# The adaLN slabs of a hybrid decoder layer between the slabs of its input projection, on one Trainium2 core

## The chip, the cores and the metric

The kernel runs on one core of a Trainium2 chip. The metric is device time in microseconds (us) of a whole call, a launch of one program; the median of several runs is given. The profile is that of one execution, and durations below are taken from it. Engines are named as in the profile: PE is TensorE (its matmuls; PEld is its weight load), DVE is VectorE, ACT is ScalarE, POOL is GpSimd, SP is SyncE, whose queue issues the weight loads. L560 is line 560 of the kernel; after the change the same code stands some 17 to 20 lines further down.

## The reference

One inference step of two layers. Each layer normalises its input, modulates it with rows of adaLN (a product of a condition vector with `w_ada`), projects it once (`w_in`), runs four mixers on the parts of that projection, and projects their results back (`w_out`); a feed-forward or experts follow. Cut to what matters here:

```python
def trunk_layer(x, mod, g_mix, g_ffn, lp, past, ffn):
    sh1, sc1, gt1, sh2, sc2, gt2 = [m[:, None, :] for m in jnp.split(mod.astype(x.dtype), 6, axis=-1)]
    h = rmsnorm(x, g_mix) * (1 + sc1) + sh1
    y, state = token_mixers(h, lp, past)
    x = x + gt1 * y
    h = rmsnorm(x, g_ffn) * (1 + sc2) + sh2
    x = x + gt2 * ffn(h)
    return x, state

# in token_mixers:  proj = h @ lp['w_in'];  ...four mixers (SSD, FoX, gated delta rule, MoBA)...;  y = y @ lp['w_out']
# in reference:     xp, sp = trunk_layer(xp, cp @ w_ada[l] + b_ada[l], ...)   and the same for the samples
```

The model width is 1024; `w_ada` has 6 x 1024 columns per layer. The prompt has 256 tokens, and eight samples bring one token each: 264 columns in the projection. The samples attend to cached pages of keys and values.

## The kernel before

**Slabs and the ring.** All large weights come through a ring of four slots (`ring0` to `ring3`). `plan_stream` writes the order of the loads as a list. Each entry is a slab with the number of ticks that its use makes. A tick is an increment of `tile_done`, which TensorE makes when a piece of work that reads a slab is over. SP goes through the list in order; `slab(i)` waits until the slab that held the slot before has made its last tick, then issues the load. So SP's queue is in order, and a slab that waits holds up all behind it. A program chooses the slot of each slab ahead of time, by who was used longest ago.

**The input projection.** `project` multiplies 26 tiles, 128 columns of `w_in` each, from nine slabs (`IN_SLABS`). Eight slabs hold three tiles and the third one, slab 2, holds two; they are 1.5 and 1.0 MB. A tile is 24 matmuls (L747, L748, L749): weights and input are each split into a high and a low part. ScalarE makes the high part from the ring (`in_high`, L1388), VectorE the low part (L1877). `IN_SPLITS` = 3 tiles are split ahead: in `drain`, ScalarE first splits tile j + 3 and then copies the result of tile j out of its bank (L1471). Two banks of PSUM alternate. Between tiles TensorE also runs small pieces (`sums` and `rows_fox` after tile 7, `head_norms` after tiles 13, 20 and 24), and VectorE runs the convolutions.

**An adaLN block.** A slab of `w_ada` (2 MB, 512 columns) is used by `ada_unit`, in two halves ("units") of 16 k-steps and column groups each, so that a block is 2 units; the trace has it as 64 records of L667. It writes bank 0. ScalarE copies that to `mrow` (`mod_rows`), TensorE transposes `mrow` into bank 1 (`ada_turn`, L676), ScalarE copies this on into `modT` (`mod_columns`). `ada_fill(l, place)` runs the units that the table `ADA_UNITS` gives a place, and ahead of each block the turn of the one before it; `ada_drain` does the copies at the same place of ScalarE's program. What a block makes is wanted only by the end of the mixers, by the feed-forward and by the next layer.

**What follows the projection.** The places are, in order, `gdn` (gated delta rule), `chain` (its last step), `ssd`, then `att0` to `att7`, the eight heads of attention of the prompt. Into the heads the samples' work is woven: `state_rows` (L982), `value_rows` (L990), `key_sums` (L996), `state_outputs` (L1005), `cache_bias`. For each head TensorE computes the scores (`score`, L953 and L954), VectorE reads them and makes the weights (`shares`, L2083 to L2085), TensorE turns them (`turn_shares`, L644) and multiplies the values (`values`, L970 to L972). The cache pages come through the same ring: `k` (two loads of a page set, without a tick) and `v`, and in the samples' attention they are used.

Before the change layer 0 has 1 block at `gdn`, 1 at `chain`, 2 at `ssd` and 1 at each of `att0` to `att6`; layer 1 has 1, 1, 1 and 1 at each of `att0` to `att3`.

Of the kernel before, what the change touches and what calls it, by code (L numbers as in the profile page):

```python
# [30 lines left out]
P = 128  # L31
# [5 lines left out]
DEPTH = 2  # L37
# [23 lines left out]
NSLOT = 4  # L61
# [17 lines left out]
def consts():  # L79
# [49 lines left out]
    {"gdn": 2, "chain": 2, "ssd": 4, **{f"att{n}": 2 for n in range(7)}, "att7": 0},  # L129
    {"gdn": 2, "chain": 2, "ssd": 2, **{f"att{n}": 2 for n in range(4)}, **{f"att{n}": 0 for n in range(4, 8)}}]  # L130
# [11 lines left out]
def plan_stream():  # L142

    out = [("ada", 0, (c,), 1) for c in range(MIX_CHUNKS)]
    for l in range(DEPTH):
        if l:
            out += [("ada",) + (NORM_ADA["mix", l][0], (NORM_ADA["mix", l][1],), 1)]
        out += [("in", l, s, s[1] // P) for s in IN_SLABS]
        ada = [("ada", la, (c,), 1) for la, c in MIXER_ADA[l]]
        out += ada[:NSLOT] + [("k", l, (m,), 0) for m in range(2)] + ada[NSLOT:] + [("v", l, (m,), 1) for m in range(2)]  # L150
        out += [("out", l, (c,), 4) for c in range(2)]
        if l == 0:
            out += [("ada",) + (NORM_ADA["ffn", l][0], (NORM_ADA["ffn", l][1],), 1)]
            out += [("gu", l, (c,), 4) for c in range(FF // 256)]
            out += [("down", l, (c, h), 4) for c in range(4) for h in range(2)]
    return out

def build(nc, A, O, const_at, NCONST):
    ctx = ExitStack()  # L160
    with ctx:
# [346 lines left out]

        class Order:
# [119 lines left out]
        def _(pe):  # L629
# [29 lines left out]
            def ada_unit(l, c, half):  # L659

                w = ring[slot_of[index[("ada", l, c)]]][:, :].rearrange("p (k n) -> p k n", k=KD)
                if half == 0:
                    use(index[("ada", l, c)])
                b = fill(0, "mod_rows") if half == 0 else bank[0]
                for k in range(4 * half, 4 * half + 4):
                    for j in range(4):
                        ins = mm(b[j * QUAD:(j + 1) * QUAD, 0:P], cT[:, k, :], w[:, k, j * P:(j + 1) * P],  # L667
                                 start=k == 0, stop=k == KD - 1)
                if half:
                    tick(ins)  # L670

            def ada_turn(l, c):

                o.need("mod_rows")
                b = fill(1, "mod_ready")
                pe.transpose(b[:, 0:P], mrow[:, :], C("ident")).then_inc(sem("mod_turned"), 1)  # L676
# [74 lines left out]
            def project(l, first, n):  # L751

                for t in range(first, first + n):
                    s, m = in_tiles[t]
                    if m == 0:
                        pe.wait_ge(landed[slot_of[index[("in", l) + s]]], landed_at[index[("in", l) + s]])
                    o.need("in_w_low", 1 if t else 3)
                    b = fill(tiles[0] % 2, "tile_copied")
# [278 lines left out]
            def attention(l):  # L1037
# [5 lines left out]
                for n in range(8):  # L1043
# [7 lines left out]
                    ada_fill(l, f"att{n}")  # L1051
# [286 lines left out]
            for l in range(DEPTH):  # L1338
# [19 lines left out]
                project(l, 25, 1)  # L1358
                gdn_beta_rows()
# [23 lines left out]
        def _(act_e):  # L1383
# [15 lines left out]
            def mod_rows(l, c):  # L1399
# [3 lines left out]
                copy(mrow[:, :], bank[0][:, 0:P], "mod_rows")  # L1403

            def mod_columns(l, c):
                o.need("mod_turned")
                copy(modT[:, 4 * c:4 * c + 4, :], bank[1][:, 0:P].rearrange("p (m j) -> p m j", m=4)[:, :, 0:9], "mod_ready")
# [45 lines left out]
            def in_high(l, t):  # L1453
# [4 lines left out]
                if t >= IN_SPLITS:  # L1458
                    act_e.wait_ge(tile_done, ticks_before(index[("in", l) + IN_SLABS[0]]) + t + 1 - IN_SPLITS)
                copy(win_high[:, t % IN_SPLITS, :, :], in_tile(l, t), "in_w_high")  # L1460

            def drain(l, first, n):
                i0 = ticks_before(index[("in", l) + IN_SLABS[0]])
                for j in range(first, first + n):
                    if j + IN_SPLITS < TILES:
                        in_high(l, j + IN_SPLITS)
                    act_e.wait_ge(tile_done, i0 + j + 1)
                    b = bank[(i0 + j) % 2]
# [20 lines left out]
            for l in range(DEPTH):  # L1489
# [63 lines left out]
                drain(l, 25, 1)  # L1553
                head_roots()
# [76 lines left out]
                for n in range(8):  # L1631
# [4 lines left out]
                    ada_drain(l, f"att{n}")  # L1636
# [959 lines left out]
```

## Time and profile before

| | |
|---|---|
| runs | 1411.69, 1418.78, 1423.9 us |
| median | 1418.78 us |
| span of the profiled execution | 1419.1 us |
| PE busy | 1301.8 us (92%) |
| PEld busy | 1126.2 us (79%) |
| DVE busy | 941.5 us (66%) |
| ACT busy | 707.7 us (50%) |
| DMA | 326.76 MB, 230 GB/s in the mean |

"Busy" is a share of the whole span and so a mean over stages with different limits; which engine a stage waits for is seen only when the span is cut. The chain that ended last is the work followed back from the last instruction, at each step to what released it. The input projection lies from 44 to 134 us in layer 0 and from 556 to 646 us in layer 1, the heads of attention and the samples' work within them from 207 to 281 us and from 715 to 780 us.

### The profile page before, as it was taken

To read this page: it belongs to the slowest core of one execution; us is meant where nothing else is said; L and a number is where in the kernel's file an instruction comes from. 1 tells how busy PE (TensorE), PEld (TensorE's weight loads), DVE (VectorE), ACT (ScalarE), POOL (GpSimd) and SP (SyncE) were. 2 spreads that over 40 slices of the span, in tenths; PEclk is the share of its full clock that TensorE was granted. 3 is DMA by queue.
4 is the path that set the end of the run, shared out by engine and by line. 5 is a ranking of instruction groups with operands and counts; after the bars stand their busy time and mean duration, and the time that the engine had idled before them with its cause. 6 is when DMAs were issued, how large, how long until landed. Compare 5 with 4: busy or idle time off the path is not lost.

```text
span 1419.1 us, 25438 instructions
## 1 busy us (share of the span) xinstructions
PE 1301.8 (92%) x10487; PEld 1126.2 (79%) x10487; DVE 941.5 (66%) x1612; ACT 707.7 (50%) x1188; POOL 10.1 (1%) x22
## 2 busy tenths in 40 slices
PE   4999898987999998998888878999999999999994
PEld 3899756766999997998666657888887979797984
DVE  1675635624555545676358247898899899989986
ACT  2566222214444444563132125776677677767772
POOL 0000000000000000000000000000000000000000
PEclk9999877588999999999776888999999999999997
DMA  9545358553444443456265523898889889979991
GB/s 388 213 154 207 121 183 318 180 215 149 178 179 141 164 186 130 175 202 202 62 226 163 188 110 125 324 358 304 320 336 347 301 324 351 335 281 343 349 339 39
DMA packets 30332, 326.76 MB, mean 230 GB/s; under 512 B 6018, under 2 KB 6530, under 8 KB 8066
## 3 DMA queue, kind: packets, MB, share of 16 engines
q1 hardware_dynamic: 28738, 319.17, 61.3%
q0 software_dynamic: 1472, 5.89, 1.1%
q8 instruction: 86, 1.41, 0.4%
q14 instruction: 36, 0.29, 0.1%
HBM read 319.15 MB, written 5.89 MB: 229 GB/s over the span
## 4 chain that ended last, share of the span: by engine, by line
PE 81%; DVE 9%; DMA 4%; ACT 3%; issue 3%; SPq 0%; DVEq 0%; POOL 0%; ACTq 0%; POOLq 0%
PE bank L747 19%; PE bank L748 18%; PE bank L749 18%; PE bank L1132 4%; DMA ring<-in_w_ada 4%; PE bank L667 3%; PE bank L803 2%; PE bank L1226 2%; PE bank L644 1%; PE bank L699 1%; DVE w_low L2400 1%; DVE win_low L1877 1%; PE bank L1254 1%; PE bank L1005 1%; PE bank L770 1%
## 5 line engine op out<-in xcount | busy, mean ns | idle before, releaser
L2400 DVE TENSOR_TENSOR w_low<-ring,w_high 128x1024 fp32r<-128x1024 f32 x352 | 399.6, 1172 | 46.0 <-ACT w_high L1756 44.5
L1756 ACT ACTIVATE w_high<-ring 128x1024 fp32r<-128x1024 f32 x352 | 342.2, 1016 | 15.1 <-PE bank L749 13.9
L747 PE MATMUL bank<-w_high,hcH 128*128 128x512 f32 x448 | 184.9, 413 | 2.3 <-DVE w_low L2400 1.9
L749 PE MATMUL bank<-w_low,hcH 128*128 128x512 f32 x448 | 176.2, 393 | 0.0
L748 PE MATMUL bank<-w_high,hcL 128*128 128x512 f32 x448 | 176.0, 393 | 0.0
L747 PE MATMUL bank<-w_high,hidH 128*128 128x256 f32 x448 | 128.5, 287 | 3.0 <-DVE w_low L2400 3.0
L749 PE MATMUL bank<-w_low,hidH 128*128 128x256 f32 x448 | 126.7, 283 | 0.0
L748 PE MATMUL bank<-w_high,hidL 128*128 128x256 f32 x448 | 126.7, 283 | 0.0
L747 PE MATMUL bank<-pH,win_high 128*128 128x264 f32 x416 | 119.9, 288 | 2.5 <-issue 2.0
L1388 ACT ACTIVATE arena<-bank 128x264 f32<-128x264 f32 (+8 forms) x128 | 51.7, 407 | 137.7 <-PE bank L644 51.9
L748 PE MATMUL bank<-pH,win_low 128*128 128x264 f32 x416 | 117.9, 283 | 0.0
L749 PE MATMUL bank<-pL,win_high 128*128 128x264 f32 x416 | 117.8, 283 | 0.0
L747 PEld LDWEIGHTS bank<-w_high,hcH 128*128 128x128 f32 x448 | 84.4, 188 | 37.2 <-DVE w_low L2400 22.4
L747 PE MATMUL bank<-hH,w_high 128*128 128x264 f32 x352 | 101.1, 287 | 5.0 <-DVE w_low L2277 5.0
L1388 ACT ACTIVATE w_high<-ring 128x1024 fp32r<-128x1024 f32 (+1 forms) x76 | 71.5, 944 | 63.3 <-PE bank L749 63.3
L748 PE MATMUL bank<-hH,w_low 128*128 128x264 f32 x352 | 100.8, 286 | 0.0
L749 PE MATMUL bank<-hL,w_high 128*128 128x264 f32 x352 | 100.7, 286 | 0.0
L749 PEld LDWEIGHTS bank<-w_low,hcH 128*128 128x128 f32 x448 | 84.3, 188 | 18.9
L2277 DVE TENSOR_TENSOR w_low<-ring,w_high 128x1024 fp32r<-128x1024 f32 (+1 forms) x76 | 80.0, 1081 | 28.0 <-ACT w_high L1388 28.0
L748 PEld LDWEIGHTS bank<-w_high,hcL 128*128 128x128 f32 x448 | 84.7, 189 | 13.1
L1877 DVE TENSOR_TENSOR win_low<-ring,win_high 128x1024 fp32r<-128x1024 f32 x52 | 62.9, 1222 | 42.2 <-ACT win_high L1388 30.1
L747 PEld LDWEIGHTS bank<-w_high,hidH 128*128 128x128 f32 x448 | 85.8, 192 | 3.9 <-issue 3.9
(393 smaller groups left out, 2548.5 us busy)
## 6 DMA issues: line engine op xcount, KB each, us to landing
ring<-in_moe_gu SPq DMA_DIRECT2D x56, 2048.0 KB, 8.6
ring<-in_moe_down SPq DMA_DIRECT2D x32, 1792.0 KB, 7.6
ring<-in_w_ada SPq DMA_DIRECT2D x24, 2048.0 KB, 8.9
ring<-in_w_in SPq DMA_DIRECT2D x16, 1536.0 KB, 6.5
ring<-in_ffn_gu SPq DMA_DIRECT2D x11, 2048.0 KB, 7.6
ring<-in_ffn_down SPq DMA_DIRECT2D x8, 1408.0 KB, 5.8
ring<-in_w_out SPq DMA_DIRECT2D x4, 2048.0 KB, 7.7
ring<-in_cache_fox_k SPq DMA_DIRECT2D x32, 128.0 KB, 3.0
```

The source lines that it names most:

```text
L667: ins = mm(b[j * QUAD:(j + 1) * QUAD, 0:P], cT[:, k, :], w[:, k, j * P:(j + 1) * P], start=k == 0, stop=k == KD - 1)
L747: mm(out, wh, xh, start=start, stop=False)
L748: mm(out, wl, xh, start=False, stop=False)
L749: return mm(out, wh, xl, start=False, stop=stop)
L803: ins = mm(b[q, h * HD:(h + 1) * HD], lhs(q, g * H + h), rhs(q, g * H + h), start=True, stop=True)
L1132: ins = mm(b[:, 0:NT], w[:, k, m * P:(m + 1) * P], yT[:, k, :], start=k == 0, stop=k == KD - 1)
L1226: ins = mm(bank[6 + part][:, i * 2 * CAP:(i + 1) * 2 * CAP], (htokH, htokL)[part][:, g, k * P:(k + 1) * P], G[:, g, :, :], start=g == 0, s ...
L1388: o.go(A_(out, in_, ACT.Copy), name)
L1756: A_(split(w_high), src, ACT.Copy).then_inc(sem("w_high_ready"), 1)
L1877: v(TT(win_low[:, t % IN_SPLITS, :, :], in_tile(l, t), win_high[:, t % IN_SPLITS, :, :], ALU.subtract), "in_w_low")
L2277: v(TT(split(w_low), src, split(w_high), ALU.subtract), "split_low")
L2400: TT(split(w_low), src, split(w_high), ALU.subtract).then_inc(sem("w_low_ready"), 1)
```

## The change

The blocks leave the heads. Nine places `in0` to `in8` in the projection stand for its slabs; in layer 0 a block is run after each of slabs 1 to 8, in layer 1 after each of slabs 1 to 7; in0 has none. Layer 0 keeps one block at each of `gdn`, `chain` and `ssd`, layer 1 keeps none outside the projection. In `plan_stream` the slabs of `w_ada` stand between those of `w_in` in the same order, and the rest of them follow; the pages `k`, that stood behind the fourth adaLN slab, come after the last of them, ahead of `v`. In `ada_banks` the blocks within the projection get banks 6 and 7 for their rows and turns, the others keep 0 and 1. `in_tick` works out ScalarE's ticks anew, since the blocks' ticks now stand among those of the tiles, and the bank of a tile follows the tile's number.

```diff
 ADA_UNITS = [
-    {"gdn": 2, "chain": 2, "ssd": 4, **{f"att{n}": 2 for n in range(7)}, "att7": 0},
-    {"gdn": 2, "chain": 2, "ssd": 2, **{f"att{n}": 2 for n in range(4)}, **{f"att{n}": 0 for n in range(4, 8)}}]
+    {**{f"in{n}": 2 for n in range(1, 9)}, "gdn": 2, "chain": 2, "ssd": 2},
+    {**{f"in{n}": 2 for n in range(1, 8)}, "in8": 0, "gdn": 0, "chain": 0, "ssd": 0}]
...
-        out += [("in", l, s, s[1] // P) for s in IN_SLABS]
         ada = [("ada", la, (c,), 1) for la, c in MIXER_ADA[l]]
-        out += ada[:NSLOT] + [("k", l, (m,), 0) for m in range(2)] + ada[NSLOT:] + [("v", l, (m,), 1) for m in range(2)]
+        for n, s in enumerate(IN_SLABS):
+            out += [("in", l, s, s[1] // P)]
+            k = ADA_UNITS[l][f"in{n}"] // 2 if n else 0
+            out += ada[:k]
+            ada = ada[k:]
+        out += ada + [(kind, l, (m,), t) for kind, t in (("k", 0), ("v", 1)) for m in range(2)]
         out += [("out", l, (c,), 4) for c in range(2)]
...
+        def in_tick(l, t):
+
+            s_, m = in_tiles[t]
+            return ticks_before(index[("in", l) + s_]) + m + 1
+
+        def ada_banks(l, c):
+
+            own = next(m for m in range(DEPTH) if (l, c) in MIXER_ADA[m]) if (l, c) in sum(MIXER_ADA, []) else None
+            if own is None:
+                return 0, 1
+            inside = sum(ADA_UNITS[own].get(f"in{n}", 0) for n in range(1, 9)) // 2
+            return (6, 7) if MIXER_ADA[own].index((l, c)) < inside else (0, 1)
...
                 for t in range(first, first + n):
                     s, m = in_tiles[t]
+                    if t and m == 0 and IN_SLABS.index(s) > 1:
+                        ada_fill(l, f"in{IN_SLABS.index(s) - 1}")
...
-                    ada_fill(l, f"att{n}")
...
                 project(l, 25, 1)
+                ada_fill(l, "in8")
                 gdn_beta_rows()
...
                 if t >= IN_SPLITS:
-                    act_e.wait_ge(tile_done, ticks_before(index[("in", l) + IN_SLABS[0]]) + t + 1 - IN_SPLITS)
+                    act_e.wait_ge(tile_done, in_tick(l, t - IN_SPLITS))
...
                 for j in range(first, first + n):
+                    slab_n = IN_SLABS.index(in_tiles[j][0])
+                    if in_tiles[j][1] == 0 and slab_n > 1:
+                        ada_drain(l, f"in{slab_n - 1}")
                     if j + IN_SPLITS < TILES:
                         in_high(l, j + IN_SPLITS)
...
                 drain(l, 25, 1)
+                ada_drain(l, "in8")
                 head_roots()
...
-                    ada_drain(l, f"att{n}")
```

`ada_unit`, `ada_turn`, `mod_rows` and `mod_columns` now take their bank from `ada_banks`.

In SP's queue at the start of layer 0's projection, the loads of slabs 0 to 8 of `w_in` and of the first blocks before the change (the width of a row is the number of elements per partition: 3072 is a slab of three tiles, 4096 a slab of `w_ada`):

```order
L560 DMA ring0<-in_w_in 128x3072
L560 DMA ring1<-in_w_in 128x3072
L560 DMA ring2<-in_w_in 128x2048
L560 DMA ring3<-in_w_in 128x3072
L540 DMA arena<-in_conv 128x240
L560 DMA ring0<-in_w_in 128x3072
L560 DMA ring1<-in_w_in 128x3072
L560 DMA ring2<-in_w_in 128x3072
L560 DMA ring3<-in_w_in 128x3072
L560 DMA ring0<-in_w_in 128x3072
L557 DMA ring1<-in_w_ada 128x4096
L557 DMA ring2<-in_w_ada 128x4096
```

The same place after it:

```order
L577 DMA ring0<-in_w_in 128x3072
L577 DMA ring1<-in_w_in 128x3072
L574 DMA ring2<-in_w_ada 128x4096
L577 DMA ring3<-in_w_in 128x2048
L557 DMA arena<-in_conv 128x240
L574 DMA ring0<-in_w_ada 128x4096
L577 DMA ring1<-in_w_in 128x3072
L574 DMA ring2<-in_w_ada 128x4096
L577 DMA ring3<-in_w_in 128x3072
L574 DMA ring0<-in_w_ada 128x4096
L577 DMA ring1<-in_w_in 128x3072
```

Of the four slots two now go round among the slabs of `w_in` and two among those of `w_ada`: the fourth slab of `w_in` reuses the slot of the second.

On TensorE, where tile 5 of layer 0's projection ends and tile 6 begins (slab 1 to slab 2), the rows after the change; before it the tiles follow on each other here without another row between L749 and L747:

```order
L765 MATMUL bank<-pH,win_high 128x264
L766 MATMUL bank<-pH,win_low 128x264
L767 MATMUL bank<-pL,win_high 128x264
L685 MATMUL bank<-ring,cT 32x128 x32
L765 MATMUL bank<-pH,win_high 128x264
L766 MATMUL bank<-pH,win_low 128x264
L767 MATMUL bank<-pL,win_high 128x264
```

The block (L685, both units in one row) stands between the tiles; from the next slab on the turn of the block before it (L694) stands ahead of each.

On TensorE in layer 0's heads 3 and 4, before the change (L990 is `value_rows`, L996 `key_sums`):

```order
L676 MATMUL bank<-cst,mrow 128x128
L667 MATMUL bank<-ring,cT 32x128 x32
L990 MATMUL bank<-arena,cst 64x128 x16
L644 MATMUL bank<-cst,arena 128x128 x3
L970 MATMUL bank<-arena 64x128
L971 MATMUL bank<-arena 64x128
L972 MATMUL bank<-arena 64x128
L953 MATMUL bank<-arena 128x128
L954 MATMUL bank<-arena 128x256
L676 MATMUL bank<-cst,mrow 128x128
L667 MATMUL bank<-ring,cT 32x128 x32
L996 MATMUL bank<-arena,cst 128x512 x2
```

And after it:

```order
L1010 MATMUL bank<-arena,cst 64x128 x16
L661 MATMUL bank<-cst,arena 128x128 x3
L990 MATMUL bank<-arena 64x128
L991 MATMUL bank<-arena 64x128
L992 MATMUL bank<-arena 64x128
L973 MATMUL bank<-arena 128x128
L974 MATMUL bank<-arena 128x256
L1016 MATMUL bank<-arena,cst 128x512 x2
```

Turn and block (L676, L667) are gone from between the scores of a head and the samples' work; the rest stands as it was.

## Rows read from the trace of the kernel before

**Rows 1.** Page, part 4: the chain that ended last, by engine and line.

```profile
PE 81%; DVE 9%; DMA 4%; ACT 3%; issue 3%; SPq 0%; DVEq 0%; POOL 0%; ACTq 0%; POOLq 0%
```

**Rows 2.** Windows: us; busy PE, PEld, DVE, ACT, POOL (instructions); PEclk, DMA share, GB/s.

```profile
44.40:133.80 89.40, 88.16 (x704) 86.30 (x703) 54.74 (x99) 54.02 (x113) 1.22 (x2) 1.00 0.44 162
44.40:61.65 17.25, 17.25 (x144) 17.25 (x143) 8.03 (x18) 7.61 (x18) 0.67 (x1) 1.00 0.27 98
207.03:245.54 38.51, 32.35 (x416) 23.14 (x416) 22.68 (x81) 10.18 (x37) 0.91 (x2) 0.81 0.80 295
245.54:280.70 35.16, 33.19 (x262) 25.76 (x262) 25.17 (x39) 9.18 (x29) 0.17 (x1) 0.50 0.56 173
715.09:753.04 37.95, 30.76 (x351) 21.37 (x351) 22.88 (x81) 9.80 (x35) 0.91 (x2) 0.77 0.60 204
753.04:780.25 27.21, 25.04 (x138) 19.61 (x138) 25.18 (x39) 8.21 (x25) 0.17 (x1) 0.56 0.51 152
```

**Rows 3.** Timeline of TensorE: start us, busy us, what, [idle ahead <-releaser].

```profile
139.84 1.95 PE L667 MATMUL bank<-ring,cT 128*32 128x128 f32 x64
...
237.20 0.33 PE L676 MATMUL bank<-cst,mrow 128*128 128x128 f32 x1
```

**Rows 4.** Timeline of TensorE and VectorE in layer 1's mixers, `gdn` and `chain`.

```profile
658.63 1.15 PE L803 MATMUL bank<-cst,arena 64*64 64x64 f32 x32 [1.66 <-DVE arena L1980]
...
693.82 3.64 PE L667 MATMUL bank<-ring,cT 128*32 128x128 f32 x64
...
700.63 0.55 PE L920 MATMUL bank<-arena 128*64 128x128 f32 x6
...
695.63 0.42 DVE L2034 TENSOR_TENSOR arena<-arena 64x256 f32<-64x256 f32 x1
```

**Rows 5.** Timeline of VectorE just behind layer 0's projection.

```profile
137.91 0.69 DVE L1951 TENSOR_TENSOR arena<-arena,bank 128x512 f32<-128x512 f32 x1 [1.32 <-ACT arena L1559]
```

**Rows 6.** Timeline of ScalarE in layer 0's projection, after tile 5.

```profile
62.16 1.06 ACT L1388 ACTIVATE win_high<-ring 128x1024 fp32r<-128x1024 f32 x1 [1.55 <-PE bank L749]
63.13 0.36 ACT L1471 ACTIVATE arena<-bank 128x256 f32<-128x256 f32 x1
```

**Rows 7.** Page, part 6 (us to landing), and L560's five loads of 53 to 90 us.

```profile
ring<-in_w_ada SPq DMA_DIRECT2D x24, 2048.0 KB, 8.9
...
DMA to landing us min/median/max: 6.1/6.6/7.3
```

**Rows 8.** Timeline of TensorE and VectorE around tile 14 of layer 0.

```profile
92.30 0.36 PE L747 MATMUL bank<-pH,win_high 128*128 128x264 f32 x1 [1.01 <-issue]
...
90.97 1.23 DVE L1877 TENSOR_TENSOR win_low<-ring,win_high 128x1024 fp32r<-128x1024 f32 x1 [3.79 <-ACT arena L1388]
...
94.12 1.22 DVE L1877 TENSOR_TENSOR win_low<-ring,win_high 128x1024 fp32r<-128x1024 f32 x1
```

**Rows 9.** Waits of VectorE in 207 to 245.54: us in total, times, longest.

```profile
DVE arena L2142 <- PE bank L996: 8.8, 2, 8.7
...
DVE arena L2121 <- PE bank L982: 4.1, 1, 4.1
```

**Rows 10.** Timeline of TensorE in heads 3 to 5, layer 0, then layer 1.

```profile
235.07 0.55 PE L644 MATMUL bank<-cst,arena 128*128 128x128 f32 x3
235.55 0.43 PE L970 MATMUL bank<-arena 128*64 128x128 f32 x2
...
239.55 1.98 PE L996 MATMUL bank<-arena,cst 128*128 128x512 f32 x4
...
246.43 0.69 PE L970 MATMUL bank<-arena 128*64 128x128 f32 x2
...
247.90 0.79 PE L953 MATMUL bank<-arena 64*128 64x128 f32 x2
...
743.04 1.96 PE L990 MATMUL bank<-arena,cst 8*64 8x128 f32 x32
```

**Rows 11.** Chain of waits within layer 0's heads: start us, us, what.

```profile
227.74 9.89 DMA ring<-in_w_ada
```

More of the change, by code:

```diff
@@ L663, in ada_unit @@
                     use(index[("ada", l, c)])
-                b = fill(0, "mod_rows") if half == 0 else bank[0]
+                rb = ada_banks(l, c)[0]
+                b = fill(rb, "mod_rows") if half == 0 else bank[rb]
                 for k in range(4 * half, 4 * half + 4):
@@ L674, in ada_turn @@
                 o.need("mod_rows")
-                b = fill(1, "mod_ready")
+                b = fill(ada_banks(l, c)[1], "mod_ready")
                 pe.transpose(b[:, 0:P], mrow[:, :], C("ident")).then_inc(sem("mod_turned"), 1)
@@ L757, in project @@
                     o.need("in_w_low", 1 if t else 3)
-                    b = fill(tiles[0] % 2, "tile_copied")
+                    b = fill(t % 2, "tile_copied")
                     wh, wl = win_high[:, t % IN_SPLITS, :, :], win_low[:, t % IN_SPLITS, :, :]
@@ L1402, in mod_rows @@
                 act_e.wait_ge(tile_done, ticks_before(i) + 1)
-                copy(mrow[:, :], bank[0][:, 0:P], "mod_rows")
+                copy(mrow[:, :], bank[ada_banks(l, c)[0]][:, 0:P], "mod_rows")
             def mod_columns(l, c):
                 o.need("mod_turned")
-                copy(modT[:, 4 * c:4 * c + 4, :], bank[1][:, 0:P].rearrange("p (m j) -> p m j", m=4)[:, :, 0:9], "mod_ready")
+                copy(modT[:, 4 * c:4 * c + 4, :], bank[ada_banks(l, c)[1]][:, 0:P].rearrange("p (m j) -> p m j", m=4)[:, :, 0:9], "mod_ready")
             def ada_drain(l, place):
@@ L1458, in in_high @@
                 if t >= IN_SPLITS:
-                    act_e.wait_ge(tile_done, ticks_before(index[("in", l) + IN_SLABS[0]]) + t + 1 - IN_SPLITS)
+                    act_e.wait_ge(tile_done, in_tick(l, t - IN_SPLITS))
                 copy(win_high[:, t % IN_SPLITS, :, :], in_tile(l, t), "in_w_high")
             def drain(l, first, n):
-                i0 = ticks_before(index[("in", l) + IN_SLABS[0]])
                 for j in range(first, first + n):
+                    slab_n = IN_SLABS.index(in_tiles[j][0])
+                    if in_tiles[j][1] == 0 and slab_n > 1:
+                        ada_drain(l, f"in{slab_n - 1}")
                     if j + IN_SPLITS < TILES:
                         in_high(l, j + IN_SPLITS)
-                    act_e.wait_ge(tile_done, i0 + j + 1)
-                    b = bank[(i0 + j) % 2]
+                    act_e.wait_ge(tile_done, in_tick(l, j))
+                    b = bank[j % 2]
                     kind, i = dst_of[l][j]
```

## The prediction

> **What bounds the kernel now.** I read the page's chain of waits first: 81% of the chain that ended last is TensorE, 4% the loads of adaLN slabs [rows 1]. That is a mean over stages with different limits, so I cut the span by stage. In layer 0's input projection TensorE is busy 88.2 of 89.4 us at the full clock (2.4 GHz), and the DMA queues only 0.44 [rows 2]: whatever is put on TensorE there must be paid. In the attention heads it is otherwise. I cut them at VectorE's own work: from its first read of a score to the end of `shares(3)` (first half), and from there to the row maxima of the cache scores (second half). First halves: 38.51 us in layer 0 and 37.95 in layer 1, VectorE busy 22.7 and 22.9; second halves: 35.16 and 27.21, VectorE busy 25.2 in both [rows 2]. The granted clock there is 0.81, 0.50, 0.77 and 0.56, a mixture of the two levels, 1.2 and 2.4 GHz. The second half of layer 1 has no adaLN block, that of layer 0 has two; otherwise they run the same program. So the change takes work from a stage where VectorE should be the bound, and puts it into one where TensorE is.
>
> **What is added: the projection.** A block (two units, 64 records) takes 1.95 us at the full clock, the turn of the block before it 0.33 [rows 3]; at the half clock a block takes 3.64 [rows 4]. Layer 0 gets eight blocks in its projection, layer 1 seven. The first has no turn: seven cost 1.95 + 6 x 2.28 = 15.6 us per layer on an engine that had nothing free.
>
> The eighth block of layer 0 stands behind the last tile, where ScalarE is the path: it reads the tile, takes roots, and its exponentials (L1559) release VectorE at 137.91, after VectorE has waited 1.32 us for them [rows 5]. It now has to copy the block's rows before the roots, so it waits for turn and block, 2.28, and copies for some 0.1, less the tile's own copy, 0.36 [rows 6], which lies beside: +2.0. Layer 1 has none there.
>
> **A new wait.** The ring has four slots. A slab of w_in now waits for the one two before it, not four. It lands 6.1 to 7.3 us after its issue, 6.6 in the median [rows 7]. ScalarE splits a tile three ahead *before* it empties the present bank: 1.06 us of split, then about 0.5 of copy [rows 6]. For slabs of three tiles this just fits: the slab is issued at t; TensorE runs a block (2.28) and two tiles of 24 matmuls, 0.12 us apart (144 in 17.25, [rows 2]), 2.88 each, and asks for the bank at t + 8.0; ScalarE hands it over at t + 6.6 + 1.06 + 0.4 = t + 8.1. But slab 2 has two tiles, so the split for slab 3 stands ahead of the copy of slab 1's last tile, and the slot of slab 3 is freed by that same tile. TensorE asks for the bank after a block and one tile, t + 1.95 + 2.88 = t + 4.8, and gets it at t + 6.6 + 1.06 + 0.5 = t + 8.2: +3.3 us in each layer. Behind ScalarE's wait stand VectorE's remainders of the split, and behind those the convolutions; with a block per slab they have some 2 us more than now and are not late.
>
> Against this TensorE has a little free time: 1.0 us ahead of tile 14, and from there to tile 17 it follows VectorE, whose splits come 3.15 us apart against 2.88 for a tile [rows 8]. A block before tiles 14 and 17 fills the first hole, four times 0.27, and some after it: −2.4 per layer. Per layer the projection so grows by 15.6 + 3.3 − 2.4 = 16.5; I add 1.0 in all for loads that land somewhat later because the queue now carries 2 MB more per slab. In all, layer 0: 18.5, layer 1: 16.5, and 1.0.
>
> **What is taken away before the heads.** `gdn` keeps its block in layer 0 and loses it in layer 1; there TensorE stands still for 1.66 us just after, until VectorE's mask (L1980) releases it [rows 4], so a block taken out ahead only lengthens that wait: 0. Layer 0's `ssd` goes from two blocks to one: −2.3 (turn and block). Layer 1 loses `chain` and `ssd`. The first runs at the half clock to 697.4, but what follows needs VectorE, which is ready only at 696.05; then come 1.8 us of TensorE's own work (L905, L644, turn), so the next step starts at about 697.85 in place of 700.63 [rows 4]: −2.8. `chain` of layer 0 is as before.
>
> **What is taken away in the heads.** Second half of layer 0: without its two blocks it should take what layer 1's takes: 35.16 − 27.21 = −8.0. Layer 1's stays.
>
> First halves: VectorE's own 22.8 us plus the waits that remain. The greatest of layer 0 is 8.7 us for the key sums of the delta rule in head 4 [rows 9]. They stand behind `turn_shares`, `values`, `score` and, so far, a block. Without it, at the full clock, `turn_shares` takes 0.5 us (235.07 to 235.55), `values` and `score` together 1.65 (to 237.20, [rows 3]) and the first of two sums 1.0, half of 1.98 [rows 10]; at the half clock `values` takes 1.5 (246.43 to 247.90), and all of it I put at 6.0. VectorE has 1.1 us of its own to do meanwhile, by an estimate. So it waits some 2.1 us at the full clock and 4.9 at the half one. At the half clock `value_rows`, 1.96 us at the full one [rows 10] and so 3.9, also ends after the shares are ready, by an estimate of 2.2; then 0.4 or 1.3 for the second sum. With 1.7 to 2.3 us of small waits for `state_rows`, an estimate from the 4.1 that the longest of them takes with a block ahead [rows 9]: 22.8 + 2.5 + 1.7 = 27.0 at the full clock, 22.8 + 8.4 + 2.3 = 33.5 at the half one. Before, 38.51 and 37.95. Which clock? With blocks it was 0.81 and 0.77; the heads with less work, 0.50 and 0.56 [rows 2]. I take a value in between, 31.0: −7.5 and −7.0.
>
> The rule that speaks against the change: the Trainium skill ("TensorE: Matmul & The Clock Gate", part 1) says that the throttled state is the default and that activity releases it, so that filler taken out of a waiting engine leaves it slow. By this all heads would run at 1.2 GHz, 33.5 us each, and the sum would be 5 us more. The rows bear it out only in part: two blocks in layer 0's second half did not lift 0.50.
>
> **The cache pages.** They now follow all adaLN slabs. The k pages wait for slots of blocks that are over by the end of the projection; they are wanted only in head 5, so both sides of the bound are nothing. The v pages and the slabs of w_out come earlier and are waited for by nobody. The loads that TensorE waited for in the heads (9.9 us from issue to landing on the chain, [rows 11]) lie within the first halves and are gained above, not twice.
>
> **The sum**, against the profiled execution's span of 1419.1 us, 0.3 above the runs' median of 1418.78: layer 0: 18.5 − 2.3 − 7.5 − 8.0 = +0.7. Layer 1: 16.5 − 2.8 − 7.0 = +6.7. With 1.0: +8.4. The feed-forward and the experts are untouched. Predicted: 1427 us.
>
> **The rivals.**
> *Heads at the full clock* (not slower). If TensorE, with less to do but less to wait for, keeps 2.4 GHz, first halves take 27.0: another −8, 1419 to 1420; and if the second halves' score chains go too, 2 us less in each, near VectorE's 25.2: 1416. For it: 0.81 and 0.77 with long stretches at the full clock. Against: 0.50 and 0.56 in second halves. Chance 0.27.
> *Heads at the half clock*: a TensorE that mostly waits falls to 1.2 GHz in all heads; first halves 33.5, +5: 1432. For it: layer 1's bare second half at 0.56. Chance 0.2, and I count it with the likeliest below, since it differs by less than a measurement can tell. (It is the rule of the Trainium skill named above.)
> *Slabs land late* (slower). If w_in slabs take the time of loads that share the queue, 9.9 us [rows 11] in place of 6.6, the bank comes 3.3 us late at each slab from 3 to 8, five more times in both layers and once more at slab 3: about 6 x 3.3 x 2 = 40 less what a longer period leaves the queue; +15 to +35: 1442 to 1462. It decides from a landing of 6.9 us on, the last that hides. Against it: a block's slab of 2 MB (8.9 us in the median, [rows 7]) is issued some 9 us before the next w_in slab and so has just landed. Chance 0.15.
> *The blocks hide in the projection* (faster): then some 30 us of additions fall and the time is near 1395. Against it: TensorE busy 88.2 of 89.4 us at the full clock [rows 2]. Chance 0.05.
>
> **How the numbers follow.** The likeliest, a mixed to low clock in the heads and slabs that land in time: 0.53 with the half clock, its own range 1421 to 1434. Heads at the full clock 0.27, slabs late 0.15, hidden 0.05. For 8 in 10: from 1411, below the full-clock case's 1416 by its unknowns, to 1443, where the late slabs begin. A measurement of this kernel tells about 1% (14 us). Faster than 1405: the hidden blocks and a little of the full clock: 0.08. Slower than 1433: late slabs 0.15, and 0.15 of the half clock with later landings: 0.30. Same: 0.62.
>
> **What would show it.** Right: projection of layer 0 from first tile to last 105 to 107 us instead of 89.4; TensorE idle about 3 us after tile 6 of each layer, with ScalarE's split waiting for a slab; L1559's successor 2 us later; heads without loads on the chain, first halves 27 to 34 us, second halves 27. Wrong: w_in slabs that land later than 7.5 us; second half of layer 0 above 29; a clock in the projection below 1.0; or waits for k pages in heads 5 to 7.

## The result, and the profile of the changed kernel

The changed kernel takes 1432.21 us in the median of its runs (1426.74 to 1435.8), the kernel before 1418.78. The ratio is 1.0103, with a 95% interval of 1.008 to 1.0126: slower by 1%, 13.4 us by the medians. The prediction was 1427 us, 1411 to 1443.

The profiled execution has a span of 1431.2 us. I cut it at the same places as before: the projection from its first tile to the first row of `gdn_beta_rows`, the first half of the heads from VectorE's first read of a score to the end of `shares(3)`, the second half from there to the row maxima of the cache scores. First the windows of the change that answer to [rows 2] (us; busy PE, PEld, DVE, ACT, POOL with their instructions; PEclk, DMA share, GB/s), layer 0, then layer 1:

```profile
42.65:152.08 109.43, 105.99 (x1223) 101.89 (x1221) 54.87 (x101) 56.17 (x130) 1.22 (x2) 0.98 0.72 275
...
215.74:247.79 32.05, 26.79 (x91) 16.50 (x91) 22.48 (x81) 8.23 (x27) 0.90 (x2) 0.53 0.25 70
247.79:275.00 27.21, 25.23 (x132) 19.47 (x132) 25.18 (x40) 8.23 (x25) 0.18 (x1) 0.50 0.26 97
550.73:660.85 110.12, 105.41 (x1159) 101.58 (x1157) 55.82 (x102) 55.65 (x126) 1.09 (x2) 0.97 0.63 232
...
732.38:764.74 32.36, 27.54 (x91) 16.52 (x91) 22.65 (x81) 8.23 (x27) 0.91 (x2) 0.57 0.04 16
764.74:791.94 27.20, 24.81 (x136) 19.66 (x137) 25.17 (x39) 8.30 (x25) 0.17 (x1) 0.56 0.05 20
```

The projections went from 89.4 us to 109.4 and 110.1. The first halves fell to 32.1 and 32.4, and TensorE's granted clock there is now 0.53 and 0.57, against 0.81 and 0.77 with the blocks. Layer 0's second half takes what layer 1's takes, 27.2.

The whole of it by stages, cut from the first and last rows of TensorE and VectorE (the last column is a second execution of the changed kernel, an experiment below):

| us | before | changed | changed, again |
|---|---|---|---|
| start to layer 0's first tile | 44.40 | 42.65 | 42.09 |
| layer 0: projection | 89.40 | 109.43 | 111.30 |
| gdn, to the chain | 33.48 | 33.08 | 33.84 |
| chain | 16.69 | 12.57 | 16.49 |
| chain's block, ssd, to `decode_spread` | 21.07 | 16.02 | 19.71 |
| heads, first half | 38.51 | 32.05 | 32.04 |
| heads, second half | 35.16 | 27.21 | 27.20 |
| layer 1: projection | 89.42 | 110.12 | 110.44 |
| gdn, to the chain | 34.23 | 33.49 | 34.71 |
| chain | 13.33 | 17.05 | 13.89 |
| ssd, to `decode_spread` | 19.62 | 19.01 | 18.40 |
| heads, first half | 37.95 | 32.36 | 31.57 |
| heads, second half | 27.21 | 27.20 | 27.21 |

What is not in the table moved by less than 1 us in the first execution. In sum layer 0 gained 5.8 us, 1.75 of it ahead of its first tile, and layer 1 lost 17.0.

The new wait stands where it was looked for. TensorE in layer 0 between tile 6 and tile 7 and for a while after, then the same place of layer 1 (start, us busy, what, [idle ahead <- releaser]):

```profile
64.91 0.28 PE L766 MATMUL bank<-pH,win_low 128*128 128x264 f32 x1
...
68.36 0.56 PE L765 MATMUL bank<-pH,win_high 128*128 128x264 f32 x1 [3.05 <-ACT arena L1408]
68.72 0.42 PE L766 MATMUL bank<-pH,win_low 128*128 128x264 f32 x1
...
71.30 0.29 PE L766 MATMUL bank<-pH,win_low 128*128 128x264 f32 x1
...
577.29 0.56 PE L765 MATMUL bank<-pH,win_high 128*128 128x264 f32 x1 [3.90 <-ACT arena L1408]
```

ScalarE at that place of layer 0 (L1408 splits, L1493 copies the bank; they were L1388 and L1471):

```profile
66.82 1.06 ACT L1408 ACTIVATE win_high<-ring 128x1024 fp32r<-128x1024 f32 x1 [7.95 <-DMA ring<-in_w_in]
67.78 0.37 ACT L1493 ACTIVATE arena<-bank 128x256 f32<-128x256 f32 x1
```

ScalarE waits 7.95 us for slab 3, splits its first tile, and only then empties the bank that TensorE wants for tile 7. TensorE stands still for 3.05 us, in layer 1 for 3.90. And then there is something that the prediction did not have: a matmul behind the wait takes 0.42 us until 71, and 0.29 after it. The granted clock was 1.00 ahead of the wait and 0.50 when TensorE started again, so the next work ran at 1.2 GHz.

The loads of w_in (six per layer, from issue to landing) were hardly slower than the 6.1, 6.6 and 7.3 of [rows 7]; layer 0, then layer 1:

```profile
L577 SPq DMA_DIRECT2D ring<-in_w_in x6: 327/328/332, 60.4 to 122.6; - x6
...
DMA to landing us min/median/max: 6.1/6.4/7.5
```

```profile
L577 SPq DMA_DIRECT2D ring<-in_w_in x6: 327/328/328, 568.4 to 633.9; - x6
...
DMA to landing us min/median/max: 6.1/6.7/7.6
```

### The profile page after: what moved, and what is told of

The parts are those of the page before. It is cut to its first block, busy times and chain, and to the rows that moved or that the text cites. A ratio compares the mean times of both kernels' runs of the same rounds, so it can differ in the third digit from the quotient of the medians.

```text
span 1431.2 us, 25436 instructions
## 1 busy us (share of the span) xinstructions
PE 1308.0 (91%) x10487; PEld 1130.4 (79%) x10487; DVE 941.6 (66%) x1612; ACT 705.0 (49%) x1188; POOL 10.1 (1%) x22
## 4 chain that ended last, share of the span: by engine, by line
PE 82%; DVE 8%; DMA 3%; ACT 3%; issue 3%; SPq 0%; DVEq 0%; POOL 0%; ACTq 0%; POOLq 0%
PE bank L765 19%; PE bank L766 18%; PE bank L767 18%; PE bank L1151 4%; PE bank L685 2%; PE bank L823 2%; DMA ring<-in_w_ada 2%; PE bank L1245 2%; DMA ring<-in_w_in 1%; PE bank L661 1%; PE bank L717 1%; PE bank L790 1%; DVE w_low L2422 1%; PE bank L1273 1%; PE bank L1025 1%
## 5 line engine op out<-in xcount | busy, mean ns | idle before, releaser
L1778 ACT ACTIVATE w_high<-ring 128x1024 fp32r<-128x1024 f32 x352 | 342.2, 1016 | 15.1 <-PE bank L767 13.9
L1408 ACT ACTIVATE arena<-bank 128x264 f32<-128x264 f32 (+8 forms) x128 | 51.7, 408 | 167.8 <-PE bank L661 72.4
L1408 ACT ACTIVATE w_high<-ring 128x1024 fp32r<-128x1024 f32 (+1 forms) x76 | 71.5, 945 | 63.3 <-PE bank L767 63.3
L1408 ACT ACTIVATE win_high<-ring 128x1024 fp32r<-128x1024 f32 x52 | 54.6, 1058 | 77.5 <-DMA ring<-in_w_in 39.8
```

The lines of the kernel that those rows point to most:

```text
L1408: o.go(A_(out, in_, ACT.Copy), name)
L1778: A_(split(w_high), src, ACT.Copy).then_inc(sem("w_high_ready"), 1)
```

## The experiments

**The same kernel again** (no edit).

> The changed kernel once more, unaltered. In its first profile the last step of the delta rule (chain) took 12.57 us at a granted clock of 0.85 in layer 0 and 17.04 us at 0.54 in layer 1; before the change it was the other way round, 16.69 at 0.56 and 13.33 at 0.79. If the program sets the clock there (what stands ahead of it in each layer), this run shows the same two times within 0.5 us. If the clock's fall comes at a moment that the program does not set, they come out otherwise, by up to 4 us each. The projections (109.4 and 110.1 us) and the heads' second halves (27.2) should repeat within 0.5 us by either.

Windows over the chain, layer 0 and layer 1, of before, of the change, and of the change again:

```profile
167.28:183.97 16.69, 14.99 (x81) 10.40 (x81) 0.66 (x2) 2.65 (x8) 0.00 (x0) 0.56 0.00 1
680.15:693.48 13.33, 11.64 (x81) 7.66 (x81) 0.66 (x2) 2.65 (x8) 0.00 (x0) 0.79 0.01 2
```

```profile
185.16:197.73 12.57, 10.88 (x81) 7.37 (x81) 0.66 (x2) 2.65 (x8) 0.00 (x0) 0.85 0.19 53
...
694.33:711.38 17.05, 15.36 (x82) 10.76 (x82) 0.66 (x2) 2.65 (x8) 0.00 (x0) 0.54 0.10 29
```

```profile
187.23:203.72 16.49, 14.80 (x81) 10.24 (x81) 0.66 (x2) 2.65 (x8) 0.00 (x0) 0.57 0.14 37
...
701.88:715.77 13.89, 12.20 (x82) 8.11 (x82) 0.66 (x2) 2.65 (x8) 0.00 (x0) 0.74 0.03 11
```

The two layers changed places with one and the same program. So the chain's 4 us are not the change's doing: the clock falls somewhere in this stage, at a moment that, by these two executions, the program does not set. Over all kernels here the chain took 12.4 to 13.9 us or 16.2 to 17.1, in either layer, and nothing in between. The heads' halves, the ssd stage of layer 1 and its projection do repeat, within 0.8 us; layer 0's projection came out 1.9 longer, more than expected, and its ssd stage 3.7.

**Work in the wait, put badly.**

```diff
                     o.need("in_w_low", 1 if t else 3)
+                    if t == 7:
+                        pe.wait_ge(*owner[6])
+                        for k in range(12):
+                            for j in range(4):
+                                mm(bank[6][j * QUAD:(j + 1) * QUAD, P:2 * P], cT[:, k % KD, :], C("ident"),
+                                   start=k == 0, stop=k == 11)
```

> The changed kernel with 48 small matmuls (constants that are in place, into a part of a bank that nobody reads) on TensorE ahead of tile 7 of each layer's projection, where it now stands still for slab 3: some 2.9 us of work at the full clock in a wait of 3.1 to 3.9. Theory that the wait costs twice, once for the slab and once because the clock has fallen to 1.2 GHz when TensorE starts again (tile 7 and what follows took 1.9 us longer than at 2.4 GHz in layer 0, 3.0 in layer 1): tile 7 starts when it did, at the full clock, and the projections fall from 109.4 to 107.5 us and from 110.1 to 107.1. Rival: the slow stretch behind the wait has nothing to do with the wait; the projections stay within 0.5 us, or grow by what the small matmuls overrun.

It tells nothing on the question. Bank 6 holds the rows of the first block, and ScalarE copies them behind its wait for slab 3. So the filling waited as tile 7 did, and was done late, at the half clock (96 records, 0.043 us each):

```profile
69.22 4.12 PE L782 MATMUL bank<-cst,cT 128*32 128x128 f32 x96 [3.20 <-ACT mrow L1414]
```

Layer 0's projection grew to 113.6 us. After 3.20 us of standing still the next matmuls ran at the half clock once more. The whole took 1450.41 us in its one execution; of the 17 us that its profile is longer than that of the changed kernel the two projections hold 5.1, and the rest lies behind them (4.5 in layer 0's chain).

**Work in the wait, mended:** the same, into bank 7.

> As the run before, but the 48 small matmuls go to another bank, whose last reader is long done: there they waited themselves for ScalarE's copy of the block's rows, which stands behind the wait for slab 3, so TensorE stood still as before and then did them at the half clock (4.1 us). Now nothing holds them: they fill the wait ahead of tile 7, 2.9 of its 3.1 to 3.9 us. Theory that the wait costs twice, by the slab and by the clock that has fallen when TensorE starts again: tile 7 starts when it did, at the full clock; the projections fall from 109.4 to 107.5 us and from 110.1 to 107.1. Rival: the slow stretch has nothing to do with the wait; the projections stay within 0.5 us.

```profile
65.81 2.83 PE L783 MATMUL bank<-cst,cT 128*32 128x128 f32 x96
69.44 0.39 PE L765 MATMUL bank<-pH,win_high 128*128 128x264 f32 x1 [0.80 <-ACT arena L1415]
```

Its projections, whole:

```profile
43.22:152.54 109.32, 107.62 (x1319) 103.16 (x1317) 54.95 (x99) 56.42 (x130) 1.22 (x2) 1.00 0.71 274
...
556.34:663.17 106.83, 105.36 (x1254) 101.40 (x1253) 55.77 (x102) 55.41 (x126) 1.09 (x2) 1.00 0.65 241
```

The granted clock is 1.00 throughout. From the start of tile 7 to that of tile 8 (with `sums`, `rows_fox` and a block between) it is 9.3 us in both layers, against 10.6 and 12.0 in the changed kernel and 11.8 and 11.9 in its repetition: the fallen clock had cost 1.3 to 2.7 us. Layer 1's projection fell by 3.3, near the 3.0 expected, but not by the clock alone: slab 3 landed after 6.2 us and not 7.3, so that tile 7 began 1.2 us earlier, tile 13 did not wait, and a new wait of 1.5 at tile 19 took some of it back. Layer 0's stayed, against the expectation: its tile 7 began 0.5 us later than in the first execution, tile 13 waited 0.5, and the loss to be saved there was only 1.3; against the repetition it is 2.0 shorter. The whole took 1432.52 us, in one execution.

One more run bears on this. The run with a block's work in the heads, below, has the change's own projection, with nothing in the wait. In layer 0 TensorE stood still for 3.14 us ahead of tile 7, and the clock did not fall:

```profile
68.56 0.36 PE L765 MATMUL bank<-pH,win_high 128*128 128x264 f32 x1 [3.14 <-ACT arena L1414]
68.75 0.28 PE L766 MATMUL bank<-pH,win_low 128*128 128x264 f32 x1
```

From tile 7 to tile 8 it took 9.3 us there, as with the wait filled; in its layer 1, after 3.13 us, it took 10.7. So of six unfilled waits five cost twice, by their length of 3.05 to 3.90 us and by 1.3 to 2.7 us of a fallen clock, and one cost its length alone: 3.13 us let the clock fall and 3.14 did not, so the length alone does not decide it. With the wait filled nothing was lost behind it, in either layer; nor was it where the wait is gone altogether, in the next experiment (9.1 us from tile 7 to tile 8 in both layers, with a block and no turn). That the wait is what brings the second cost is so shown; that filling it saves that cost is likely, but each layer has only one such execution, and in layer 1 the wait would have been 1.2 us shorter than the 3.90 of the changed kernel anyway.

**The edge between slabs 1 and 2 without a block.**

```diff
-    {**{f"in{n}": 2 for n in range(1, 9)}, "gdn": 2, "chain": 2, "ssd": 2},
-    {**{f"in{n}": 2 for n in range(1, 8)}, "in8": 0, "gdn": 0, "chain": 0, "ssd": 0}]
+    {"in1": 0, **{f"in{n}": 2 for n in range(2, 9)}, "gdn": 2, "chain": 2, "ssd": 4},
+    {"in1": 0, **{f"in{n}": 2 for n in range(2, 9)}, "gdn": 0, "chain": 0, "ssd": 0}]
```

> The changed kernel without a block on the edge between slabs 1 and 2: layer 0 does it in its ssd place (two blocks there, as before the change), layer 1 behind the last slab (in8). Theory of the wait for slab 3: TensorE's stall after tile 6 (some 4.9 us in layer 0, 6.9 in layer 1 by the spacing of the tiles) is gone, because slab 3 then takes the slot of slab 0 and is issued a slab earlier. Layer 0's projection, to the first row of beta, goes from 109.4 to 102.5 (4.9 and a block of 2.0 less), its ssd stage gains 2.3 to 5; layer 1's goes from 110.1 to 103.2 and its step behind it grows by 2.0. In all 1422 to 1425 us. Rival: the queue with 2 MB more per slab is what is slow, landings take over 7 us and the stall moves to another edge; the projections shrink by no more than the block of 2 us, 1430 to 1433 us.

Measured: 1425.78 us, 1.0069 of before (1.0036 to 1.0101), which took 1418.06 us in the median of the same set of runs. Projections 104.2 and 106.5 us. The wait ahead of tile 7 is gone in both layers. But a part of it came back, above all in layer 1, where slab 7 landed late (the load that was issued at 614.6 us) and tile 19 waited:

```profile
624.73 0.36 PE L765 MATMUL bank<-pH,win_high 128*128 128x264 f32 x1 [2.22 <-ACT arena L1408]
```

```profile
DMA to landing us min/median/max: 8.7/8.7/8.7
```

Right on the cause of the wait; the time is 1 us over what was expected, since a stall did move to another edge, as the rival had it. Why that load took 8.7 us stays open: a slab of `w_ada` had been issued 2 us after it, but one was issued 2 us after a load in the changed kernel, too, that landed after 6.3 us (layer 0, issued at 88.0).

**Thin blocks.**

```diff
-                for k in range(4 * half, 4 * half + 4):
+                for k in (range(4 * half, 4 * half + 4) if rb == 0 else range(KD - half, KD)):
...
-                                 start=k == 0, stop=k == KD - 1)
+                                 start=k == 0 or rb > 0, stop=k == KD - 1)
```

> The changed kernel with the blocks inside the projection cut to their last 4 of 32 matmuls (the loads, the ticks, the copies and the turns stay; the adaLN rows that they make are not the reference's). By the price of TensorE's work alone, 8 blocks of 1.95 us become 0.25: layer 0's projection falls by 13.6 from 109.4 to 95.8, layer 1's by 11.9 from 110.1 to 98.2. By the theory that the ring sets the pace as soon as the blocks are shorter, TensorE asks for the bank at each slab 1.7 us earlier and finds it 1.7 us not ready (slab issued, 6.6 us to land, 1.06 of split, 0.4 of copy: 8.1, against 0.6 of turn and thin block and 5.76 of two tiles): nearly all comes back as stalls at slabs 3 to 8, and the projections stay at 105 to 109 us.

```profile
43.57:147.27 103.70, 94.85 (x775) 90.00 (x773) 54.91 (x99) 56.11 (x130) 1.21 (x2) 0.98 0.73 283
...
548.58:653.70 105.12, 95.27 (x767) 90.84 (x765) 54.96 (x101) 55.28 (x126) 1.09 (x2) 0.97 0.64 240
```

TensorE's waits in layer 0's projection (us in total, times, longest):

```profile
PE bank L765 <- ACT arena L1408: 7.9, 4, 4.6
```

13.6 and 11.9 us of matmuls were taken out, and 5.7 and 5.0 came off the projections (the whole took 1422.37 us, in one execution). More than half came back as waits for slabs and a fallen clock behind them. In layer 0 they stood at four places, not six. So where the two kinds of slabs take turns, cheaper blocks alone do not make the projection short again: the ring sets its pace as much as TensorE does.

**The blocks' work in the heads without its loads.**

```diff
                         state_rows(1)
+                    if n < (7, 4)[l]:
+                        pe.wait_ge(*owner[0])
+                        for k in range(KD):
+                            for j in range(4):
+                                mm(bank[0][j * QUAD:(j + 1) * QUAD, P:2 * P], cT[:, k, :], C("ident"),
+                                   start=k == 0, stop=k == KD - 1)
                     if n == 1:
```

> The changed kernel with a block's 32 matmuls, on constants that are in place already and into a part of a bank that nobody reads, at the places in the heads where the blocks stood before (heads 0 to 6 in layer 0, 0 to 3 in layer 1): the blocks' work without loads, copies and turns. Theory that the blocks' work keeps the clock up: the granted clock in the heads' first halves rises from 0.53 and 0.57 towards the 0.81 and 0.77 of before, and the first halves (32.1 and 32.4 us now) grow by less than 2 us in spite of 5 and 4 blocks. Theory that work costs what it takes and the clock does not follow it: they grow by 1.95 to 3.6 us for each block that TensorE does not have free, to some 36 to 38 us, with the clock below 0.65; layer 0's second half goes from 27.2 back to some 34 by either, since two blocks did not lift 0.50 there.

First and second half of layer 0, first half of layer 1:

```profile
217.85:253.56 35.71, 31.02 (x411) 22.79 (x411) 22.68 (x81) 8.12 (x27) 0.91 (x2) 0.81 0.15 46
253.56:285.29 31.73, 27.72 (x260) 22.09 (x260) 25.16 (x39) 8.11 (x25) 0.17 (x1) 0.63 0.22 84
...
739.83:770.45 30.62, 25.93 (x347) 18.91 (x347) 22.67 (x81) 8.12 (x27) 0.91 (x2) 0.89 0.05 19
```

The clock follows the work: 0.53 to 0.81 and 0.57 to 0.89. In layer 1 the first half with four blocks' matmuls was 1.7 us *shorter* than without, and 1.0 shorter than in the repetition (31.57). In layer 0 five cost 3.7 us, 0.7 each, and two in the second half 4.5: neither theory alone. In the second half the clock, 0.63, is no higher than the 0.62 of the repetition without work: there it did not follow. With the real blocks the first halves had been 38.5 and 38.0. So in layer 1 the blocks' dearest part is not their matmuls; it leaves the loads, the copies and the turns. This is one execution; as a whole it took 1434.52 us.

**The cache pages last, in layer 1 alone, on the kernel before.**

```diff
-        out += ada[:NSLOT] + [("k", l, (m,), 0) for m in range(2)] + ada[NSLOT:] + [("v", l, (m,), 1) for m in range(2)]
+        first = len(ada) if l else NSLOT
+        out += ada[:first] + [("k", l, (m,), 0) for m in range(2)] + ada[first:] + [("v", l, (m,), 1) for m in range(2)]
```

> The kernel before with one part of the change alone, in layer 1 only: its cache pages k stand behind all adaLN slabs in the loads; every block stays where it was before (gdn, chain, ssd, heads 0 to 3). The k pages then no longer hold two of the four slots while the blocks of the heads are loaded. Theory that what the blocks cost in the heads is their late loads, since the same matmuls without loads left layer 1's first half at 30.6 us against 37.95 with them: the slabs of heads 0 to 3 have landed when TensorE asks, no wait on a load of w_ada is left there, and layer 1's first half falls to 30 to 33 us; the k pages are issued from the ssd stage on, land before head 5 asks, and the second half stays 27.2. In all 1411 to 1414 us. Rival: the heads pay for the blocks' matmuls and copies, not the loads; the first half stays above 35 us, 1416 to 1420 us. Second rival: the k pages come late, the second half of layer 1 grows past 29 us, and nothing is gained.

Measured: 1408.12 us, 0.9945 of before (0.992 to 0.9971). The kernel before took 1413.8 us in the median of the same set of runs, so the gain is 5.7 us by the medians and 7.8 by the ratio; that the time lies below the expected range is owed to that lower start. TensorE's waits for loads in layer 1's first half before the change, which are gone here, and then this kernel's two halves:

```profile
PE bank L667 <- DMA ring<-in_w_ada: 2.5, 2, 2.1
```

```profile
705.88:737.44 31.56, 26.87 (x351) 19.21 (x351) 22.68 (x81) 9.73 (x35) 0.90 (x2) 0.88 0.57 151
737.44:764.64 27.20, 24.64 (x142) 19.24 (x142) 25.17 (x40) 9.04 (x27) 0.17 (x1) 0.64 0.63 175
```

37.95 became 31.56. The waits themselves were 2.5 us; the rest comes with a clock of 0.88 instead of 0.77. The next run, with the pages last as well, repeats it (31.54). The k pages were not late.

**A mixture of what paid.**

```diff
+    {**{f"in{n}": 2 * (n in (4, 5, 6, 7)) for n in range(1, 9)}, "gdn": 2, "chain": 2, "ssd": 2, **{f"att{n}": 2 * (n < 4) for n in range(8)}},
+    {**{f"in{n}": 0 for n in range(1, 9)}, "gdn": 2, "chain": 2, "ssd": 2, **{f"att{n}": 2 * (n < 4) for n in range(8)}}]
...
+                    ada_fill(l, f"att{n}")
...
+                    ada_drain(l, f"att{n}")
```

> A version made of what the runs so far show: in layer 0 blocks stand between the slabs only where slabs 0 to 3 are over (in4 to in7, four blocks), one each at gdn, chain and ssd, and one at each of heads 0 to 3; layer 1 has none in its projection and keeps those of before (gdn, chain, ssd, heads 0 to 3). The cache pages follow all adaLN slabs, as in the change. By the theories of the ring and of the late loads: layer 0's projection 89.4 + 4 x 2.28 less up to 2.4 of the hole ahead of tile 14 = 96 to 99 us without a stall at tile 7; its first half 30 to 33 us (38.5 before), its second half 27.2 (35.2 before); its ssd stage one block less than before; layer 1's projection 89.4, its first half 30 to 33, its second half 27.2. Sum against before: 8 - 2 - 6.5 - 8 - 6.5 = -15, 1401 to 1407 us. Rival, that a block costs some 2 us wherever it stands and the clock takes the rest: 1414 to 1420 us.

Measured: 1404.44 us, 0.9924 of before (0.9888 to 0.9959). The range of 1401 to 1407 was met with luck: it stood for 15 us less than before, and against the 1413.8 of this set of runs the gain is 9.4 us by the medians and 10.7 by the ratio. It beats both kernels; whether it beats the run with the pages alone, the intervals do not tell. Layer 0's projection, first and second half, and layer 1's first half:

```profile
42.76:139.69 96.93, 95.82 (x964) 93.26 (x963) 55.28 (x102) 54.67 (x120) 1.21 (x2) 1.00 0.63 242
...
207.87:242.61 34.74, 30.05 (x351) 21.32 (x351) 22.78 (x81) 9.90 (x35) 0.90 (x2) 0.79 0.52 155
242.61:269.81 27.20, 24.59 (x142) 19.21 (x142) 25.17 (x40) 9.06 (x27) 0.18 (x1) 0.64 0.82 230
...
702.50:734.04 31.54, 26.86 (x351) 19.17 (x351) 22.68 (x81) 9.74 (x35) 0.90 (x2) 0.88 0.53 153
```

These stages came out as expected but for layer 0's first half, 34.7 us instead of 30 to 33, at a clock of 0.79 against 0.88 in layer 1; TensorE waited for no load there, and why it is longer stays open. The 8 us expected from layer 0's second half hold against the first profile only (see the heads, below).

## Why the prediction was right, and where its terms were off

**The blocks in the projection, and the new wait.** The mechanism, its place and its size were right: without the wait tile 7 would have begun 22.4 us after tile 0 (tile 6 at 19.5 and 2.9 for a tile), and it began at 25.7 in layer 0, 3.3 later as worked out, and at 26.6 in layer 1, 4.2 later, because slab 3 landed after 7.3 us there and not 6.6. The edge without a block took it away. The step that was off is that the clock was held at 1.0 in the whole projection: behind five of the six unfilled waits it was down, which cost another 1.3 to 2.7 us. The runs in which the wait was filled or gone lost nothing there. With the wait's own 0.9 more than forecast and 0.8 us ahead of tile 13, less 0.7 that `gdn` gained, this is why layer 1's projection and `gdn` grew by 20.0 us and not by some 17. In layer 0 the two grew by 19.6, against 18.5 and half of the 1.0 for late landings.

Two of the prediction's own signs of being wrong came true here: a clock below 1.0 in the projection (0.98 and 0.97), and in layer 1 a load that landed after 7.6 us, later than 7.5. And one of its readings does not follow from its figures: with the bank asked for at t + 8.0 and 1.06 + 0.4 us of ScalarE's work, the last landing that hides is 6.5 us, not 6.9. In layer 1 slab 5 landed after 7.2 us, and TensorE waited 0.81 us at tile 13, which puts it at 6.4.

The Trainium skill ("TensorE: Matmul & The Clock Gate", "HAM oscillation — how this bites in real kernels") describes this: a wait throttles the array again, and the work behind it runs slowly. The trace agrees in layer 0 of the changed kernel, with 0.42 us for a matmul after the wait and 0.29 later; the wait of 3.14 us in the run with work in the heads, with 0.28 us behind it, shows that it need not happen.

**The heads.** The second half of layer 0 was predicted at −8.0 and fell by 7.96. That the size came out so well is partly luck. Layer 0's program is the same in the kernel before and in the run with the pages last in layer 1 alone, and there this half, with its two blocks, took 30.65 us at a clock of 0.67:

```profile
241.44:272.09 30.65, 26.64 (x262) 20.49 (x262) 25.17 (x40) 9.05 (x29) 0.17 (x1) 0.67 0.57 172
```

So taking the two blocks out is worth 3.4 us against one execution and 8.0 against the other, and the 35.16 at 0.50 that the prediction read, and its remark that two blocks did not lift 0.50, rest on a single one. The first halves were taken at 31.0 between 27.0 and 33.5, and came out at 32.1 and 32.4, near the end of the half clock. VectorE's longest wait there is for the key sums; layer 0 (us in total, times, longest), which answers to [rows 9]:

```profile
DVE arena L2164 <- PE bank L1016: 8.4, 2, 7.3
```

That is the 7.1 us (4.9 + 2.2) that the prediction worked out for 1.2 GHz. So in this the rival of the half clock was the truer one: the granted clock was 0.53 and 0.57, and the run with filling showed that it falls because the work was taken away. The rule of the Trainium skill that the prediction weighed ("TensorE: Matmul & The Clock Gate", part 1) holds in the first halves: with a block's work put back the clock was 0.81 and 0.89.

**The mixers.** Layer 1's `chain` and `ssd` blocks were to give back 2.8 us; the stage fell by 0.6, in the repetition by 1.2. What the blocks took they had nearly paid for with the clock: the windows of before and of the change from the chain's end to `decode_spread` have 0.70 and 0.51.

```profile
693.48:713.10 19.62, 17.61 (x197) 12.20 (x196) 7.96 (x28) 4.45 (x12) 1.08 (x2) 0.70 0.54 167
```

```profile
711.38:730.39 19.01, 14.61 (x66) 8.82 (x66) 8.05 (x28) 3.61 (x8) 1.08 (x2) 0.51 0.02 7
```

In layer 0 the `ssd` stage was to fall by 2.3; it fell by 5.1 in one execution and by 1.4 in the other, with clocks of 0.90 and 0.67. The chain, put down as unchanged, moved by −4.1 and +3.7 in the profiled execution, which the repetition showed to be chance.

**The cache pages.** For this change the price of nothing was right: no load is left in the heads for which TensorE waits. But it is no small thing by itself: with the blocks left in layer 1's heads the pages' new place is worth 6.4 us there. The prediction, which cost it at nothing from both sides, looked only at whether the pages themselves come late, not at the slots that they give free.

**The sum.** Measured less predicted, in the profiled execution: layer 0's projection and gdn +0.6, its start −1.75, chain −4.1, ssd −2.8, first half +1.0; layer 1's projection and gdn +3.0, chain +3.7, ssd +2.2, first half +1.4, the rest +0.4: 3.7 us more than the +8.4 forecast, which makes the +12.1 of the two profiled executions (+13.4 in the medians). Much of the nearness is luck, since terms of both signs cancel, the chain's −4.1 and +3.7 above all. Of the rivals, late slabs did not come true (6.4 and 6.7 us in the median, not 9.9), and hidden blocks did not either.

## What to carry to other kernels

Before work is moved out of a stage that waits, look at what it waits for there: here the blocks' matmuls cost nothing in the first half of layer 1's heads, and a better place for the loads gained 6.4 us in that stage without moving any work. Work that is put between the slabs of a stream shares the stream's slots: count how many slabs ahead the ring still is at each edge, above all at a short slab. And a wait on TensorE can cost twice, by its length and by the clock after it: here the second part came to between nothing and 2.7 us for waits of 3.05 to 3.90 us.

## What the hardware showed that was not expected

After a single stop of 3.05 us, in a stage that had run at 2.4 GHz for 20 us, the matmuls ran at 1.2 GHz, for 1.3 us of loss (2.7 after a stop of 3.90); in another execution, after a stop of 3.14 us at the same place, they ran at 2.4 GHz. With 2.83 us of small matmuls in the stop, and 0.8 of it left, the clock stayed at 1.00. The clock in the chain changed from one execution to the other of one program (0.85 and 0.57 in layer 0, 0.54 and 0.74 in layer 1) and moved that stage between about 13 and 17 us, by itself a quarter of a per cent of the whole. And a stage was faster with matmuls whose results nobody reads: layer 1's first half took 30.6 us with them, 32.4 and 31.6 in two executions without.
